# A two-layer trunk on one Trainium2 core: the block trips of the second half of a layer issued from GpSimd's queue instead of SyncE's, with later take-up points

## The reference

```python
for l in range(DEPTH):                                   # DEPTH = 2
    h = rmsnorm(x, norm_mix[l])
    qa, ka, va, qi, ki, wi, qb, kb, vb = split(h @ w_in[l])
    o_a = dsa_branch(qa, ka, va, qi, ki, wi, bias_a)      # 8 heads, top-64 keys chosen by an indexer
    o_b = swa_branch(qb, kb, vb, sinks[l], bias_b)        # 16 heads, window of two chunks
    g_a, g_b = split(sigmoid(h @ w_gate[l]))
    merged = g_a * (o_a @ w_branch_a[l]) + g_b * (o_b @ w_branch_b[l])
    x = x + merged @ w_out[l]
    h = rmsnorm(x, norm_mlp[l])
    x = x + square(relu(h @ w_up[l])) @ w_down[l]         # 2048 -> 8192 -> 2048
return rmsnorm(x, final_norm)
```

## Time and profile before

| | |
|---|---|
| median of three runs | 2736.19 us (2735.28 to 2736.83) |
| time of the profiled execution | 2735.0 us |
| its span, first to last instruction | 2733.2 us |
| PE busy in the span | 2693.2 us |
| DVE, ACT, POOL busy | 1912.0, 1404.5, 45.2 us |
| mean granted clock of PE | 0.999 |
| DMA | 575.72 MB, mean 211 GB/s |
| weight load, issue to landing | 4.2 us median, 928 of them |
| store and fetch of a trip, issue to landing | 2.8 and 3.4 us median |

### The profile page before, as it was taken

How to read it: one execution, slowest core, us unless ns; L and a number is a source line. 1 busy time by engine, 2 the same in 40 slices (tenths; PEclk the granted TensorE clock), 3 DMA queues, 4 the chain that set the end, 5 groups by cost and what they waited for, 6 DMA issues and landing times.

```text
span 2733.2 us, 36575 instructions
## 1 busy us (share of the span) xinstructions
PE 2693.2 (99%) x13134; PEld 2223.7 (81%) x13134; DVE 1912.0 (70%) x2786; ACT 1404.5 (51%) x1799; POOL 45.2 (2%) x70
## 2 busy tenths in 40 slices
PE   9999999999999999999999999999999999999998
PEld 8788778887888888887887887788878887887886
DVE  5665555566788797887656656555667987978875
ACT  5545554445555555555455455444455555555553
POOL 1100000000000000001000000000000000000000
PEclk9999999999999999999999999999999999999999
DMA  8875546676666666668766654566677566666664
GB/s 261 239 225 169 177 162 199 220 224 223 223 212 211 222 209 225 213 202 240 237 229 211 209 188 160 164 205 219 220 247 237 201 216 208 208 209 212 204 230 155
DMA packets 191500, 575.72 MB, mean 211 GB/s; under 512 B 23016, under 2 KB 58388, under 8 KB 191184
## 3 DMA queue, kind: packets, MB, share of 16 engines
q1 hardware_dynamic: 188000, 568.67, 63.4%
q0 software_dynamic: 2928, 4.51, 0.8%
q10 hardware_dynamic: 384, 0.11, 0.0%
HBM read 535.15 MB, written 38.04 MB: 210 GB/s over the span
## 4 chain that ended last, share of the span: by engine, by line
PE 73%; DVE 10%; DMA 8%; issue 5%; ACT 3%; SPq 2%; DVEq 0%; ACTq 0%; POOLq 0%; POOL 0%
PE acc L473 21%; PE acc L475 20%; PE acc L474 20%; DMA raw<-in_w_main 4%; DMA scratch<-spread 3%; DVE w_lo L1166 2%; DVE w_lo L1187 1%; SPq L304 1%; PE att L441 1%; PE att L443 1%; PE att L442 1%; PE acc L441 1%; PE acc L443 1%; PE acc L442 1%; DMA moved<-scratch 1%
## 5 line engine op out<-in xcount | busy, mean ns | idle before, releaser
L1166 DVE TENSOR_TENSOR w_lo<-raw,w_hi 128x1024 fp32r<-128x1024 f32 (+1 forms) x824 | 989.0, 1213 | 509.7 <-ACT w_hi L789 507.7
L789 ACT ACTIVATE w_hi<-raw 128x1024 fp32r<-128x1024 f32 (+1 forms) x824 | 858.4, 1050 | 686.0 <-PE acc L475 524.5
L473 PE MATMUL acc<-w_hi,h_hl 128*128 128x512 f32 x2008 | 800.5, 399 | 2.2 <-DVE w_lo L1166 1.7
L475 PE MATMUL acc<-w_hi,h_hl 128*128 128x512 f32 x2008 | 792.4, 395 | 0.0
L474 PE MATMUL acc<-w_lo,h_hl 128*128 128x512 f32 x2008 | 792.0, 394 | 0.0
L473 PEld LDWEIGHTS acc<-w_hi,h_hl 128*128 128x128 f32 x2008 | 378.2, 188 | 95.3 <-issue 5.8
L475 PEld LDWEIGHTS acc<-w_hi,h_hl 128*128 128x128 f32 x2008 | 377.9, 188 | 88.8
L474 PEld LDWEIGHTS acc<-w_lo,h_hl 128*128 128x128 f32 x2008 | 378.3, 188 | 84.7
L473 PE MATMUL acc<-w_hi,o_hl 128*128 128x512 f32 x1064 | 423.5, 398 | 8.9 <-DVE w_lo L1166 6.6
L474 PE MATMUL acc<-w_lo,o_hl 128*128 128x512 f32 x1064 | 419.8, 395 | 0.0
L475 PE MATMUL acc<-w_hi,o_hl 128*128 128x512 f32 x1064 | 419.8, 395 | 0.0
(11 more groups left out here) (262 smaller groups left out, 2680.6 us busy)
## 6 DMA issues: line engine op xcount, KB each, us to landing
raw<-in_w_main SPq DMA_DIRECT2D x928, 512.0 KB, 4.2
scratch<-spread SPq DMA_DIRECT2D x67, 512.0 KB, 2.8
...
```

Source lines behind the costliest of these rows:

```text
L473: nc.tensor.matmul(o, a_hi, hi[:, kk], start=(k == 0), stop=False)
L475: last = nc.tensor.matmul(o, a_lo, hi[:, kk], start=False, stop=fin)
L789: nc.scalar.activation(w_hi[s][:, 0:2 * width], raw[r][:, 0:2 * width], ACT.Copy).then_inc(hi_ready, 1)
L1166: nc.vector.tensor_tensor(w_lo[s][:, 0:2 * width], raw[r][:, 0:2 * width], w_hi[s][:, 0:2 * width].bitcast(F32), ALU.subtract).then_inc(lo ...
```

## The change

- The trips `E_M`, `E_XO` and `E_U` (24 of the 36 or 33 of a layer) are issued by POOL: the same store and the same four fetches, with semaphores of their own (`pool_stored`, `pool_landed`). SP keeps the trips of the input projections and `E_XD`, and issues nothing but weight loads in between.
- POOL's program is written out by layer: biases, norm factor, four mixer trips, zeroing `rest`, four trips of x, norm factor, sixteen trips of the MLP. The biases of the second layer are loaded after the last of these trips; before, they were loaded beside them.
- The blocks `E_XO` + 0 to 2 are taken up a unit later: after split 1 of the unit behind, with their sums after split 2. PE's wait for `E_XO` + 2 moves from chunk 0 to chunk 4 of the unit at C_MLP.
- In the MLP the two blocks that were turned ahead of split 4 are turned ahead of split 6 (ACT's squaring goes from ahead of split 4 to ahead of 5), and the third up block is taken up after split 2 instead of 1.

```diff
@@ -234,6 +235,14 @@
         spread_ready = sem("spread_ready")
         spread_stored = sem("spread_stored")
         landed = sem("landed")
+        pool_stored = sem("pool_stored")
+        pool_landed = sem("pool_landed")
+
+        def landing(l, e, g=0):
+            if E_M <= e < E_XD:
+                return pool_landed, g * (NBLK * LANDED) + (l * POOL_MOVES + (e - E_M + 1)) * LANDED
+            return landed, (l * (MOVES - POOL_MOVES) + (e - (POOL_MOVES if e >= E_XD else 0) + 2)) * LANDED
+
         placed = sem("placed")
         moved_hi = sem("moved_hi")
         moved_took = sem("moved_took")
...
 
-            def pass_on(l, e, g=0, pieces=PIECES):
+            def pass_on(l, e, pieces=PIECES):
 
                 size = pieces * TT * 32
                 dst = moved[:, 0:QUARTERS * size].rearrange("p (i e) -> p i e", i=QUARTERS)
 
                 def store():
-                    sp.wait_ge(spread_ready, g * NBLK + (l * MOVES + e + 1))
+                    sp.wait_ge(spread_ready, l * MOVES + e + 1)
                     sp.dma_start(bass.AP(scratch, 0, [[NB * TT, P], [1, QUARTERS * size]]),
                                  spread[:].rearrange("p j k t s -> p (j k t s)")[:, 0:QUARTERS * size]).then_inc(spread_stored, 16)
 
                 def fetch():
-                    sp.wait_ge(spread_stored, g * (NBLK * 16) + (l * (MOVES * 16) + (e + 1) * 16))
+                    sp.wait_ge(spread_stored, (l * (MOVES - POOL_MOVES) + e - (POOL_MOVES if e >= E_XD else 0) + 1) * 16)
                     for jj in range(QUARTERS):
                         sp.dma_start(dst[32 * jj:32 * jj + 32],
                                      bass.AP(scratch, jj * size, [[NB * TT, 32], [32 * NB * TT, QUARTERS], [1, size]]))\
@@ -317,10 +326,10 @@
                     load_unit(l, C_MIXA + 12 * n, 8, pass_on(l, E_QB + 1) if n == 0 else None)
                     load_unit(l, C_MIXA + 12 * n + 8, 4)
                 for n in range(NBLK):
-                    load_unit(l, C_MIXB + 12 * n, 8, pass_on(l, E_M + n - 1) if n else None)
+                    load_unit(l, C_MIXB + 12 * n, 8)
                     load_unit(l, C_MIXB + 12 * n + 8, 4)
                 for n in range(NBLK):
-                    load_unit(l, C_OUT + 8 * n, 8, pass_on(l, E_XO + n - 1) if n else pass_on(l, E_M + 3))
+                    load_unit(l, C_OUT + 8 * n, 8)
 
                 def load_up(g, n, passing=None):
...
@@ -328,22 +337,21 @@
                 def load_down(g, n, passing=None):
                     load_unit(l, g * 64 + (C_MLP + 32 + 8 * n), 8, passing)
 
-                load_up(0, 0, pass_on(l, E_XO + 3))
+                load_up(0, 0)
                 if l == DEPTH - 1:
                     sp.wait_ge(mixed, NBLK * DEPTH)
                     sp.dma_start(last_gain, final_gain).then_inc(final_loaded, 16)
-                load_up(0, 1, pass_on(l, E_U))
+                load_up(0, 1)
                 with sp.Fori(0, GROUPS - 1) as g:
-                    load_up(g, 2, pass_on(l, E_U + 1, g))
-                    load_up(g, 3, pass_on(l, E_U + 2, g))
-                    load_unit(l, g * 64 + (C_MLP + 32), 8, pass_on(l, E_U + 3, g), g * 64 + (C_MLP + 64))
+                    load_up(g, 2)
+                    load_up(g, 3)
+                    load_unit(l, g * 64 + (C_MLP + 32), 8, None, g * 64 + (C_MLP + 64))
...
+
+                size = NB // QUARTERS * TT
+                pool.wait_ge(spread_ready, l * MOVES + e + 1)
+                pool.dma_start(bass.AP(scratch, 0, [[NB * TT, P], [1, NB * TT]]),
+                               spread[:].rearrange("p j k t s -> p (j k t s)")).then_inc(pool_stored, 16)
+                pool.wait_ge(pool_stored, (l * POOL_MOVES + e - E_M + 1) * 16)
+                dst = moved[:].rearrange("p (i e) -> p i e", i=QUARTERS)
+                for jj in range(QUARTERS):
+                    pool.dma_start(dst[32 * jj:32 * jj + 32],
+                                   bass.AP(scratch, jj * size, [[NB * TT, 32], [32 * NB * TT, QUARTERS], [1, size]]))\
+                        .then_inc(pool_landed, 16)
+
+            def factor(i):
                 pool.wait_ge(mean_ready, i + 1)
                 power()
+
+            for l in range(DEPTH):
+                load_bias_b(l)
+                if l:
+                    factor(2 * l)
+                for n in range(NBLK):
+                    pass_on(l, E_M + n)
+                pool.wait_ge(mixed, (l + 1) * NBLK)
+                nc.gpsimd.memset(rest[:], 0.0).then_inc(rest_zero, 1)
+                for n in range(NBLK):
+                    pass_on(l, E_XO + n)
+                pool.wait_ge(rest_zero, l + 1)
+                factor(2 * l + 1)
+                pass_on(l, E_U)
+                for n in range(1, GROUPS * NBLK):
+                    pass_on(l, E_U + n)
+                if l < DEPTH - 1:
+                    pool.wait_ge(multiplied, l * CHUNKS + C_MLP + 64 * (GROUPS - 1) + 24 + SLOTS)
+            for t in range(TT):
+                factor(2 * DEPTH + t)
 
 
         @block.tensor
...
                 def u_sums_took(g, n):
                     return g * NBLK + (l * U_SUMS + n + 1)
 
-                up(C_MLP, 0, adds(0, -1), 0, [(0, moved_took, took_of(E_XO + 2)), (6, moved_took, took_of(E_XO + 3))])
+                up(C_MLP, 0, adds(0, -1), 0, [(0, moved_took, took_of(E_XO + 1)), (4, moved_took, took_of(E_XO + 2)), (6, moved_took, took_of(E_XO + 3))])
                 up(C_MLP + 8, 1, adds(0, 0), 1, [(0, h_sums_took, H_SUMS * (l + 1))])
                 with pe.Fori(0, GROUPS - 1) as g:
...
                          take=lambda n=n: take_gate(l * CHUNKS + (C_MIXB + 12 * n + 8), l * DVE_UNITS + (4 + n)))
 
 
+                def x_hi(n):
+                    hi_moved_x(l, E_XO + n, n, 2 * l + 1)
+
+                def h_sums(n):
+                    act.wait_ge(h_summed, l * H_SUMS + n + 1)
+                    nc.scalar.activation(s_hh[:, 0, n, :], sums_f, ACT.Copy).then_inc(h_sums_hi, 1)
+
                 for n in range(NBLK):
-                    def out_moved(n=n):
-                        if n == 0:
-                            hi_moved(l, E_M + 3, m_dst(3, 0))
-                        else:
-                            hi_moved_x(l, E_XO + n - 1, n - 1, 2 * l + 1)
-
                     def x_squares(n=n):
                         act.wait_ge(dve_took, l * DVE_UNITS + (8 + n + 1))
                         square_block(n - 1, l * (2 * NBLK) + (NBLK + n - 1))
-                    def h_sums(n=n):
-                        act.wait_ge(h_summed, l * H_SUMS + n)
-                        nc.scalar.activation(s_hh[:, 0, n - 1, :], sums_f, ACT.Copy).then_inc(h_sums_hi, 1)
-                    unit(l * CHUNKS + (C_OUT + 8 * n), 8, take=x_squares if n else None, taken=out_moved,
-                         sums=h_sums if n else None)
+                    then = {6: lambda: hi_moved(l, E_M + 3, m_dst(3, 0))} if n == 0 else \
+                        {1: lambda n=n: x_hi(n - 2), 2: lambda n=n: h_sums(n - 2)} if n >= 2 else ()
+                    unit(l * CHUNKS + (C_OUT + 8 * n), 8, take=x_squares if n else None, then=then)
 
 
                 def take_side(g, n, end):
...
@@ -1106,18 +1136,18 @@
                     return g * 2 + (l * LAYER_SIDES + i + 1)
 
                 base = l * CHUNKS + C_MLP
-                run(C_MLP, {3: last_square}, {6: lambda: hi_moved_x(l, E_XO + 3, 3, 2 * l + 1)})
+                run(C_MLP, {3: last_square}, {1: lambda: x_hi(2), 2: lambda: h_sums(2), 6: lambda: x_hi(3)})
                 run(C_MLP + 8, {3: lambda: take_up(0, 0, base + 8, 0)}, {6: lambda: u_moved(0, 0), 7: lambda: u_sums_hi(0, 0)})
                 with act.Fori(0, GROUPS - 1) as g:
                     run(g * 64 + (C_MLP + 16), {3: lambda: take_up(g, 1, g * 64 + (base + 16), 1)}, (),
                         WIDE_UP[2], steps_at(g, AT_UP2))
                     run(g * 64 + (C_MLP + 24),
-                        {3: lambda: take_side(g, 2, g * 64 + (base + 24)), 4: lambda: take_summed(g, 2, sides_count(g, 0))},
+                        {3: lambda: take_side(g, 2, g * 64 + (base + 24)), 5: lambda: take_summed(g, 2, sides_count(g, 0))},
                         {1: lambda: u_moved(g, 1), 2: lambda: u_sums_hi(g, 1)})
                     run(g * 64 + (C_MLP + 32), {3: lambda: take_up(g, 3, g * 64 + (base + 32), 1)},
-                        {1: lambda: u_moved(g, 2), 2: lambda: u_sums_hi(g, 2)}, WIDE_UP[0], steps_at(g, AT_UP0))
+                        {2: lambda: u_moved(g, 2), 3: lambda: u_sums_hi(g, 2)}, WIDE_UP[0], steps_at(g, AT_UP0))
                     run(g * 64 + (C_MLP + 40),
-                        {3: lambda: take_side(g, 4, g * 64 + (base + 40)), 4: lambda: take_summed(g, 4, sides_count(g, 1))},
+                        {3: lambda: take_side(g, 4, g * 64 + (base + 40)), 5: lambda: take_summed(g, 4, sides_count(g, 1))},
                         {1: lambda: u_moved(g, 3), 2: lambda: u_sums_hi(g, 3)}, WIDE[0], steps_at(g, WIDE_AT[0]))
```

(8 more changed lines are left out.)

57 lines of the change are left out of this document (24 added, 33 removed).

## The result

The changed kernel takes 2755.42 us (median of 4 runs, 2753.79 to 2763.44) against 2736.27 of the kernel before, a ratio of 1.0076 with a 95% interval of 1.0056 to 1.0096. It is 19 us slower, where the prediction had 2721 and a range of 2702 to 2741. The profiled execution took 2755.8 us.

The account below looks back on a forecast made before the run. PE, busy 2693.2 of 2733.2 us, was taken as the bound, with 39 us of stalls exposed. From 2735.0, gains of 22 + 5.5 + 2.5 less losses of 15 gave 2720, as a median 2721; range 2702 to 2741.

Parts of the forecast that it names:

- The trip itself on POOL, 9.0 us: Store and four fetches issued by POOL: 9.0 us without anything else, against 7.5 us from SP.
- A wait inside POOL, in one trip of two: POOL's fetches 2 to 4: one trip in two meets a wait without semaphore, about 4 us, making 13 us.
- every trip waits: Rival, POOL's trips: each meets a wait or slow landings, 13.5 us each; 2750 us in all; chance 0.13.
- The sign that I had named: POOL's trips: a mean of about 12.5 us or more decides for the rival that every trip waits.
- SP loses 24 trips a layer, 22 us: MLP loops: loads no longer queue behind a store and fetches; three quarters of 30 us of stalls won, 22 us.
- `E_XO` + 0 to 2 a unit later, 5.5 us: C_OUT in both layers: the later take-up removes the stall behind `E_XO` + 2, 5.5 us won.
- Transposes two chunks later, nothing: MLP: transposes two splits later cost nothing; only DVE's wait for ACT's squaring goes.
- The biases and the end of layer 0's MLP, 2.5 us: End of layer 0's MLP: trips no longer share DMA engines with layer 1's bias loads, 2.5 us won.
- Where a longer trip costs: Short-notice blocks and `E_U` + 2 kinds: PE pays from ACT waits of 3.3, 5 or 6.5 us; together 15 us.
- DVE starves POOL: Rival, POOL's DMAs: DVE's work holds them up, trips of 12 to 13 us throughout; 2740 us; chance 0.05.
- the rule itself that the forecast cited: Skill page on SBUF: a DMA from GpSimd starves for descriptors while DVE runs in a two-port mode; about 2740 us.
- What would show it: Profile after: fewer SP store waits, ACT's `raw` waits under half of 132.5 us, loop idle below 10 us, new stalls.

Follow-up runs that it names:

- held runs: The changed kernel with SP's raw loads held until POOL has issued its fetches, in the MLP loops too (ratio 0.9989) or at short-notice trips alone (0.9966).
- e2: The kernel before with take-ups and transposes as changed but all trips on SP's queue: 2719.10 us, ratio 0.9928.
- e6: The kernel before with the MLP transposes later alone, their store moved, all trips on SP's queue: 2706.08 us, ratio 0.9921.
- short hold: The changed kernel with SP's raw loads held until POOL has issued its fetches, at short-notice trips alone: 2718.76 us, ratio 0.9966.

## Why the prediction was wrong, point by point

- **The trip itself on POOL, 9.0 us**: right as the price of an undisturbed trip (9.0 and 8.9 us in the held runs), in part by luck. The 7.5 us from which it started is 8.5 in the trace, because the median landing of all four fetches (3.4 us) was taken for that of the last one (4.1), and POOL's extra is 0.5 us, not 1.5. But no trip of the changed kernel at short notice was undisturbed.
- **A wait inside POOL, in one trip of two**: this step failed. POOL never stood still between a store's landing and its four fetches; in the changed kernel no idle time without a semaphore ends at the fetches. The pattern of the earlier trace rows didn't carry over: in the changed kernel bias loads still show such waits, eight times, and trips never. All 14 short-notice trips took 9.9 to 15.0 us, 12.5 in the mean, and most of what lengthened them was the landing, by crowding. Over the stretches outside the loops where trips moved (460 to 702 and 1828 to 2070) the kernel took 36.0 us more; the forecast had 8 us of losses there and 5.5 of gain. My rival "every trip waits" gave 2750 from a mean trip of about 12.5 us: its number came near, 2755, its mechanism was as wrong as the forecast's. The sign that I had named, over 12.5 us in the mean, was just missed: 12.5 for the short-notice trips, 11.8 from transposes to landing over all 48.
- **The missing link** is in the forecast's own argument. It said that SP, freed of trips, issues loads earlier, and priced that as gain only. The loads it frees are 2 MB beside the fetch of 0.5 MB at `E_XO` + 3, and 1.8 MB of raw packets in the mean of the 14. The contrast was there to be asked for: on SP's queue the loads stand behind the fetch by order of issue, on two queues nothing ordered them until the hold did. The Trainium skill, DMA: Bandwidth & Descriptors, section "Issuing engines are not separate DMA queues", states that DMAs from different engines run on the same 16 DMA engines and interleave. The DMA view at 668 to 674 agrees: 9.7 us for a load and 7.7 for a fetch there, against medians of 4.2 and 3.4 before.
- **SP loses 24 trips a layer, 22 us**: the size came near, the attribution is open. The loops of the changed kernel are 19.5 us shorter, longer trips included, but they have the late transposes too, which alone gain 22. The queue alone in the loops gave 13.6 (timed) to 19 us (profile) in one run and 2.9 (profile) in another.
- **`E_XO` + 0 to 2 a unit later, 5.5 us**: failed. The stall at 649 was seen in one execution, behind one long trip of 11.7 us; two kernels with the same code there have 8.3 us for that trip and no stall. The part has a cost too. The third block's take-up and sums now come right before the transposes of `E_XO` + 3, which end at 656.65 instead of 652.77 with PE equally far, and its take-up waits longer. First the run with late transposes only, then the one with the x part added, 652 to 680:

```profile
ACT h_hl L865 <- DMA moved<-scratch: 2.5, 1, 2.5
```

```profile
ACT h_hl L865 <- DMA moved<-scratch: 6.1, 1, 6.1
...
PE acc L476 <- DVE h_hl L1279: 3.0, 1, 3.0
```

  The table has 5.7 us for it there (4.9 against -0.8), 3.4 with the x part alone (2.6 against -0.8), and no gain at C_OUT that the other runs lack. The timing of the x part alone, 0.1% slower, fits a small cost without a gain.
- **Transposes two chunks later, nothing**: failed by the most. Alone they gained 0.8%, 22 us, which no version beat. DVE's waits for `raw` fell to 28.3 us by them and to 28.4 by the loops' queue alone: both take the same waits away, so the two are alternatives. I only priced the notice they cost, and one wait of DVE, not what they do to the order of DVE's splits. Whether the gain comes from the transposes or from SP's store standing before load 2 of the next unit instead of before load 7 wasn't tried apart on SP's queue; the late transposes need the store moved there. On POOL's queue, where no store of SP is left in the loops, the transposes alone gained 0.5% (1.0179 to 1.0128), so they are at least part of it.
- **The biases and the end of layer 0's MLP, 2.5 us**: not tested by itself. The stretch from 1305 to 1828, where the biases of layer 1 now arrive, grew by 0.9 us. The 25 us before 1305, where the gain was to be, shrank by 0.7; the runs e2 and e6, with the biases where they were, shrank by 1.4 there, so the gain is not seen.
- **Where a longer trip costs**: the points at which PE starts to pay roughly fit. In the mixer of layer 0 ACT waited 5.1, 7.6, 6.7 and 8.7 us. By the points (6.5 for the first three, 5 for `E_M` + 3) that is 1.1 + 0.2 + 3.7 = 5.0 us, and the table has 7.6. `E_XO` + 3 with a wait of 11.0 us costs PE 7.9, as 11.0 - 3.3 = 7.7 would have it. The clock behind it was left out of the price: 12 matmuls follow at 0.43 us apart instead of 0.23, 2.4 us more, and set against the kernel before the lag grows by 10.4 us at this one block, of the 13.6 in the stretch.
- **DVE starves POOL**: no sign, though trips of 12 to 13 us came as this rival had them. The issue took 550 to 578 ns over all 192 fetches, and landings came back to 2.9 us with DVE's work unchanged. In which mode DVE's instructions ran, no run shows, so nothing is said here of the rule itself that the forecast cited.
- **What would show it**: SP's waits for stores fell to 35.7 us in 21 trips, as said. ACT's for `raw` fell to 98.0, not below 66. PE's idle time in the windows of the loops was to fall below 10 us and is 23.2, though part of that is the shift of the windows. The other signs named (landings of 3 to 4.5 us, "issue" waits before half of the trips) didn't come: the store's 3.2 us fits, the fetch's 4.9 doesn't.

**What is left open**: what keeps a fetch at the rate below, how much of the late-transposes edit is the store's new place, and how much the queue alone gives in the loops.

The best ratio is that of the kernel before with the late transposes alone, 0.9921, from which 0.9926 and 0.9928 can't be told apart. The changed kernel can be made faster than the kernel before (0.9966 with the short hold), but its schedule on SP's queue has 0.9928, so no run shows the queue move itself to pay once the transposes are late.
